# A decoder trunk on one core: early zero fills, bias ahead of the gates on VectorE, replicas in buffers of their own

## What is computed

```python
def conformer_conv(x, w1, b1, dw, dwb, g, bn, w2, b2):
    h = x @ w1 + b1
    a, gate = jnp.split(h, 2, axis=-1)
    h = a * jax.nn.sigmoid(gate)
    h = lax.conv_general_dilated(h, dw[:, None, :], window_strides=(1,),
        padding=[(CONV_WIDTH - 1, 0)], feature_group_count=D_MODEL, ...) + dwb
    h = jax.nn.silu(layer_norm(h, g, bn))
    return h @ w2 + b2

x = layer_norm(ALPHA * x + conformer_conv(x, ...), g, b)      # ALPHA = (2 * DEPTH) ** 0.25
```

## Time and profile before

| | us |
|---|---|
| median of 3 runs | 1181.94 |
| lowest and highest run | 1174.9, 1182.1 |
| span of the profiled execution, first to last instruction | 1188.2 |
| TensorE busy | 953.6 (80%) |
| VectorE busy | 454.7 (38%) |
| GpSimd busy | 221.3 (19%) |
| ScalarE busy | 169.3 (14%) |

### The profile page before, as it was taken

The page is one execution under the profiler, slowest core; times in us unless marked ns, Lnnn a source line. Parts: engine busy times, 40 slices in busy tenths (PEclk is TensorE's granted clock), DMA queues, the critical chain, the costliest instruction groups (busy, mean ns, idle before and its releaser), DMA issues.

```text
span 1188.2 us, 13863 instructions
## 1 busy us (share of the span) xinstructions
PE 953.6 (80%) x5241; PEld 495.3 (42%) x5241; DVE 454.7 (38%) x925; ACT 169.3 (14%) x376; POOL 221.3 (19%) x314
## 2 busy tenths in 40 slices
PE   5999969983999798996478999868459957899930
PEld 3444324542554454552234454534335534455510
DVE  1799913552111111110676448564511111111126
ACT  0000021301000000000123232432020000000010
POOL 1094000024211111200330002021240211020022
PEclk8999989875999899999579899877769989999975
DMA  8994349965999999999600003201859999999932
GB/s 257 388 410 142 87 157 412 408 248 200 345 388 408 385 376 391 383 420 401 249 1 0 1 1 142 71 1 50 324 200 389 378 366 384 381 389 392 395 127 106
DMA packets 82494, 313.40 MB, mean 264 GB/s; under 512 B 8798, under 2 KB 19210, under 8 KB 74089
## 3 DMA queue, kind: packets, MB, share of 16 engines
q1 hardware_dynamic: 44944, 228.83, 50.8%
q10 hardware_dynamic: 27352, 55.35, 12.4%
q0 software_dynamic: 10112, 28.06, 6.8%
HBM read 252.48 MB, written 55.31 MB: 259 GB/s over the span
## 4 chain that ended last, share of the span: by engine, by line
PE 57%; DMA 18%; DVE 14%; issue 4%; POOL 2%; ACT 2%; SPq 1%; POOLq 0%; ACTq 0%; DVEq 0%
PE ps L604 20%; PE ps L614 10%; DVE arena L858 7%; PE ps L710 6%; PE ps L729 5%; PE ps L549 5%; DMA wring<-in_moe_w_up_dram 5%; DMA wring<-in_moe_w_gate_dram 5%; DMA arena<-in_moe_w_up_dram 3%; PE ps L507 2%; DMA wring<-in_conv_w_dram 1%; DMA arena<-xs_dram,place_i 1%; DMA xs_dram<-x_sb,place_i 1%; PE ps L755 1%; PE ps L767 1%
## 5 line engine op out<-in xcount | busy, mean ns | idle before, releaser
L604 PE MATMUL ps<-wring,arena 128*64 128x256 f32 x2016 | 241.2, 396 | 54.8 <-DVE arena L1010 31.2
L604 PEld LDWEIGHTS ps<-wring,arena 128*64 128x64 f32 x2016 | 149.6, 143 | 147.0 <-issue 57.8
L1525 POOL DMA_DIRECT2D arena<-xs_dram x172 | 91.6, 538 | 358.4 <-DVE arena L1010 334.9
L614 PE MATMUL ps<-wring,arena 128*64 128x512 f32 x560 | 126.7, 594 | 6.2 <-DVE arena L1045 5.7
L507 PE MATMUL ps<-arena,wring 128*128 128x512 f32 x256 | 112.1, 600 | 5.3 <-DMA wring<-in_conv_w_dram 5.3
L1031 DVE COPY arena<-ps 128x256 f32<-128x256 f32 x32 | 13.6, 425 | 237.2 <-PE ps L647 237.2
L858 DVE SCALAR_TENSOR_TENSOR arena<-arena,dwT 128x512 f32<-128x512 f32 x116 | 96.1, 902 | 0.0
L710 PE MATMUL ps<-wring,arena 128*128 128x512 f32 x192 | 90.9, 631 | 3.5 <-ACT arena L1373 3.5
L604 PE MATMUL ps<-arena 128*64 128x256 f32 x736 | 84.7, 385 | 9.1 <-DMA arena<-in_moe_w_up_dram 7.6
L1511 POOL TENSOR_TENSOR rstd<-vareps,half 128x1 f32<-128x1 f32 x20 | 25.7, 1287 | 284.3 <-DVE vareps L874 284.3
L507 PEld LDWEIGHTS ps<-arena,wring 128*128 128x128 f32 x256 | 49.1, 193 | 66.8 <-issue 66.8
(11 more groups left out here) (189 smaller groups left out, 896.3 us busy)
## 6 DMA issues: line engine op xcount, KB each, us to landing
wring<-in_moe_w_gate_dram SPq DMA_DIRECT2D x24, 2048.0 KB, 26.4
wring<-in_moe_w_up_dram SPq DMA_DIRECT2D x24, 2048.0 KB, 19.9
wring<-in_moe_w_down_dram SPq DMA_DIRECT2D x24, 2048.0 KB, 21.3
xs_dram<-zero ACTq DMA_DIRECT2D x2, 16384.0 KB, 64.5
arena<-in_moe_w_up_dram SPq DMA_DIRECT2D x8, 2048.0 KB, 28.0
arena<-in_moe_w_down_dram SPq DMA_DIRECT2D x8, 2048.0 KB, 19.5
arena<-in_moe_w_gate_dram SPq DMA_DIRECT2D x8, 2048.0 KB, 24.7
arena<-xs_dram POOLq DMA_DIRECT2D x172, 64.0 KB, 6.4
```

The lines of the kernel that those rows point to most:

```text
L604: mm = pe.matmul(ps[h * CAP:(h + 1) * CAP, bank, 0:256], act[:, k, :], w[:, k, h * 256:(h + 1) * 256], start=(k == 0), stop=(k == KD - 1))
L614: mm = pe.matmul(ps[h * CAP:(h + 1) * CAP, bank, :], act[:, j % 2, (j // 2) * CAP:(j // 2 + 1) * CAP], w[:, j, h * 512:(h + 1) * 512], sta ...
L1525: pool.dma_start(where[q * QROWS:(q + 1) * QROWS, :, :], xs_tiles[q, :, bass.ds(n, 1), :, :]).then_inc(signal, 16)
```

## The change

- First loads: SyncE waits for the last tile of x before it issues the weights of column tile 1. ScalarE loads only the tap columns that VectorE needs, in two pieces of 16 and 15 rows; the bias row is issued right behind the tap loads.
- VectorE divides the bias row by ALPHA and adds it to the four x tiles, ahead of the parameter copies; the factor ALPHA moves into the later addition of the product, in both layers. GpSimd's scale and addition in layer 0 go; in layer 1 GpSimd divides the row once and only adds it per tile.
- Both zero fills are issued one behind the other, after the first sigmoid.
- The replicas of all four tiles have places of their own in the three slots, so they wait for their gate alone; of tile 7, ScalarE issues eight and SyncE eight.
- The gates stand at other taps, and gate 7 behind the last tile.

```diff
             conv_in(0, 1)
+            sp.wait_ge(s_x[T - 1], 16)
             conv_in(1, 1)
...
-            replicate(4)
-            replicate(5)
-            sp.wait_ge(s_g1, KD)
-            replicate(6)
-            sp.wait_ge(s_pec, 1)
-            replicate(7)
+            for c in range(DVE_TILES, KD):
+                replicate(sp, c, (0, 1) if c == KD - 1 else (0, 1, 2, 3))
...
+        FIT = KD * F // REPW
+        def shifted(c, q):
+            slot_of, at = divmod(SHIFTS * (c - DVE_TILES) + q, FIT)
+            return wring[:, 1 + slot_of, at * REPW:(at + 1) * REPW]
...
+            dve.wait_ge(s_b2, 16)
+            own(dve.tensor_scalar(resrow, resrow, 1.0 / ALPHA, None, ALU.mult))
+            for t in range(T):
+                ins = dve.tensor_tensor(x_sb[:, t, :], x_sb[:, t, :], resrow, ALU.add)
+            own(ins)
...
-            taps(1, {4: 2, 22: 3})
-            taps(2, {7: 4, 26: 5})
-            taps(3, {10: 6, 28: 7})
+            taps(1, {5: 2, 24: 3})
+            taps(2, {11: 4, 29: 5})
+            taps(3, {16: 6})
+            glu(7)
...
-                    ins = dve.tensor_tensor(x_sb[:, t, h * 512:(h + 1) * 512], x_sb[:, t, h * 512:(h + 1) * 512],
-                                            ps[:, bank + h, :], ALU.add)
+                    ins = dve.scalar_tensor_tensor(out=half_x, in0=half_x, scalar=ALPHA, in1=ps[:, bank + h, :],
+                                                   op0=ALU.mult, op1=ALU.add)
...
-            act.dma_start(dw_r[:, :], conv_dw[0]).then_inc(s_small, 16)
+            act.dma_start(dw_r[0:16, taken_cols], conv_dw[0, 0:16, taken_cols]).then_inc(s_small, 16)
+            act.dma_start(dw_r[16:CW, taken_cols], conv_dw[0, 16:CW, taken_cols]).then_inc(s_small, 16)
...
+            act.dma_start(resrow, conv_b2[0].partition_broadcast(P)).then_inc(s_b2, 16)
...
-                clear_rows(0)
+                for i in range(2):
+                    act.dma_start(xs_halves[i], zero[:, :].unsqueeze(1).to_broadcast([P, E * S // P, 512])
+                                  ).then_inc(s_xinit, 16)
...
+                if c == KD - 1:
+                    replicate(act, c, (2, 3))
...
-            clear_rows(1)
...
-            pool.wait_ge(s_x0T, T)
-            pool.wait_ge(s_rows, 16 * 8)
-            for t in range(T):
-                own(pool.tensor_scalar(x_sb[:, t, :], x_sb[:, t, :], ALPHA, None, ALU.mult))
-                pool.tensor_tensor(x_sb[:, t, :], x_sb[:, t, :], resrow, ALU.add).then_inc(s_xa, 1)
```

More of the change, by code:

```diff
@@ L239, in trunk @@
         s_pecv = sem("s_pecv")
-        s_xa = sem("s_xa")
+        s_b2 = sem("s_b2")
         s_At = sem("s_At")
@@ L358, in trunk, with replicate @@
         wdw = wring[:, 0, :].rearrange("p (r g n) -> p r g n", r=ROUNDS, g=SHIFTS * (KD - DVE_TILES))
-        def shifted(c):
-            slot_of = (1, 2, 3, 1)[c - DVE_TILES]
-            return wring[:, slot_of, 0:SHIFTS * REPW].rearrange("p (g n) -> p g n", g=SHIFTS)
+        FIT = KD * F // REPW
+        def shifted(c, q):
+            slot_of, at = divmod(SHIFTS * (c - DVE_TILES) + q, FIT)
+            return wring[:, 1 + slot_of, at * REPW:(at + 1) * REPW]
+        def replicate(eng, c, shifts):
+            eng.wait_ge(s_glu, c + 1)
+            for s in shifts:
+                for q in range(SHIFTS):
+                    eng.dma_start(shifted(c, q)[s * GRP:(s + 1) * GRP, :],
+                                  hpad[q * GRP:(q + 1) * GRP, c, s:s + REPW]).then_inc(s_rep[c - DVE_TILES], 16)
         def slot(i, *dims):
@@ L486, in parameters @@
             def parameters():
-                pe.wait_ge(s_small, 16 * 6)
+                pe.wait_ge(s_small, 16 * 7)
                 pe.transpose(ps[:, 5, 0:NPRM], prm[:, :], ident[0:NPRM, 0:NPRM])
@@ L522, in _ @@
                                          wdw[:, r, SHIFTS * (c - DVE_TILES) + q, :],
-                                         shifted(c)[:, q, SHIFTS * r:SHIFTS * r + S],
+                                         shifted(c, q)[:, SHIFTS * r:SHIFTS * r + S],
                                          start=(r == 0), stop=(r == ROUNDS - 1))
@@ L898, in add_product @@
                 for h in range(2):
[L899 to L900 removed]
+                    half_x = x_sb[:, t, h * 512:(h + 1) * 512]
+                    ins = dve.scalar_tensor_tensor(out=half_x, in0=half_x, scalar=ALPHA, in1=ps[:, bank + h, :],
+                                                   op0=ALU.mult, op1=ALU.add)
                 ins.then_inc(signal, 1)
@@ L977, in table @@
                                   ALU.mult)
-            dve.wait_ge(s_rows, 16 * 8)
+            dve.wait_ge(s_rows, 16 * 7)
             n = 0
@@ L1140, in take @@
                     half_x = x_sb[:, t, h * 512:(h + 1) * 512]
-                    dve.tensor_tensor(half_x, half_x, ps[:, bank, :], ALU.add).then_inc(bank_read[bank - 5], 1)
+                    dve.scalar_tensor_tensor(out=half_x, in0=half_x, scalar=ALPHA, in1=ps[:, bank, :],
+                                             op0=ALU.mult, op1=ALU.add).then_inc(bank_read[bank - 5], 1)
                     if h == 1 and t == T - 1:
@@ L1456, in _ @@
             pool.memset(hpad[:, :, 0:CW - 1], 0.0).then_inc(s_pool0, 1)
-            pool.wait_ge(s_small, 16 * 6)
+            pool.wait_ge(s_small, 16 * 7)
             pool.tensor_copy(pos_f[:, :], pos_i[:, :]).then_inc(s_rope, 1)
@@ L1583, in _ @@
             pool.wait_ge(s_rows1, 16 * 5)
+            own(pool.tensor_scalar(resrow, resrow, 1.0 / ALPHA, None, ALU.mult))
             def residual(t):
```

5 lines of the change are left out of this document (1 added, 4 removed).

## The result

The changed kernel is slower: 1197.92 us median (1194.29 to 1204.55, 4 runs) against 1180.01 of the kernel before on the same chip (1174.9 to 1182.1, 4 runs). The ratio is 1.014, 95% interval 1.010 to 1.019. The forecast was 1175.0, its range 1165 to 1197. What came is rival (b), whose own time, 1198, lay just outside that range.

What follows compares the result with a forecast made beforehand. It took the end of the depthwise products (166.97 us) as the bound, with TensorE and VectorE level and the fills holding tile 7; 6.3 + 0.6 = 6.9 us off the 1181.94 median gave 1175.0, range 1165 to 1197.

Steps and rivals of the forecast that it cites:

- rival (b): ScalarE stands at the second fill's issue from 44 to near 92; depthwise end 183.6, 1198 us; chance 0.15.
- Reading of the bound: Depthwise stage: the change touches nothing on the chain from 167 to 288, so the depthwise products' end, 166.97, decides.
- Part 1: First loads: first weights come with x, start 3.8 us earlier, plus 2.0 without idle time's clock cost; 5.7 in all.
- Part 2: x and bias: some 6 us on VectorE in idle time, taken 0 cost; GpSimd loses 25.4 us of work.
- Part 3: Replicas start at each gate, 0.64 us each; with ScalarE's half in time the depthwise end is 154.1, 12.9 us earlier.
- Tiles 4 to 6 are there before TensorE asks: Replicas: copies of these tiles are ready before TensorE wants them at 126.4, 133.3 and 140.3.
- Part 4: Early fills: ScalarE's queue empties between 148.4 and 155.8, taken 151; TensorE idles 3.8 us, depthwise end 160.7, gain 6.3.
- rival (a): Fills out of the way in time, TensorE runs through to 154.1: gain 12.9 + 0.6, 1168.4 us; chance 0.23.
- the forecast's own case: Both fills early without a stand: depthwise end 160.7 instead of 167.0, gain 6.3 us.
- The term that I held to decide: ScalarE's eight tile 7 replicas queue behind both fills and land near 151, so TensorE idles 3.8 us.
- Part 5: Attention: GpSimd drops four scales and gets one; gain 0 to 1.5 us, taken 0.6.
- The best corner: Whole sum at its best: no wait, start 1.3 us sooner, 0.9 more in attention; gain 16.4, 1165.5 us.

Runs made afterwards that it cites:

- experiment 1: Changed kernel with only the second fill put back behind the four depthwise bias operations: 1172.82 us against 1182.58 before, ratio 0.991.
- experiment 3: Changed kernel with the second fill issued behind the sixth sigmoid: 1194.26 us against 1182.58 before, ratio 1.013.
- experiment 5: Changed kernel with each fill cut into eight pieces of 1024 rows, all issued at the same place: 1236.78 us against 1185.23 before, ratio 1.043.
- experiment 10: Changed kernel with the second fill issued from GpSimd's queue behind the rotary steps: 1192.96 us against 1183.76 before, ratio 1.010.
- experiment 9: experiment 1 with replicas as in the kernel before (three buffers, all on SyncE, old waits): 1173.83 us against 1183.76 before, ratio 0.992.
- experiment 2: Kernel before with only the second fill moved, issued right behind the first: 1209.4 us against 1182.58, ratio 1.026.
- experiment 11: Kernel before with only the new first loads: 1176.11 us against 1183.76, ratio 0.992.
- experiment 7: experiment 1 with the first loads as in the kernel before: 1177.42 us against 1185.23 before, ratio 0.994.
- experiment 8: experiment 1 with x and bias row on GpSimd and gates' places as before: 1174.42 us against 1185.23 before (0.989); again 1169.27 against 1183.76 (0.988).
- experiment 6: Changed kernel with fill rows of 8 KB instead of 2 KB, 2048 rows a fill, same bytes: 1187.96 us against 1185.23 before, ratio 1.003.

## Why the prediction was wrong

**Reading of the bound: right.** The depthwise end carries the result nearly one for one: -10.0 there and -9.8 in time (experiment 1), +16.6 and +17.9 (the change), +10.0 and +11.7 (experiment 3), +52.1 and +51.6 (experiment 5), +9.2 and +9.2 (experiment 10). The largest differences are 5.2 (experiment 9, -4.7 and -9.9) and 3.6 (experiment 2, +23.2 and +26.8), within the 7 us by which one kernel's later stages differ from profile to profile.

**Part 1: right in kind, at most as large as taken.** Taken 5.7 us, 3.8 at the start and 2.0 of clock. In the changed kernel 2.9 at the start (19.16 to 16.23) and 1.7 in the first tile (15.70 to 14.00), 4.6; alone (experiment 11) 5.5 at the depthwise end; taken out again (experiment 7) 2.9. The first products now wait for VectorE's copy of the transposed x and no longer for weights. The second term is not sure to come: with the new first loads and an idle time of 1.4 to 1.5 us ahead of it, the first tile took 14.00 in the changed kernel and in most experiments, but 15.6 to 15.7 in experiments 1, 5 and 9. In 1 and 9 the granted clock was 1.00 all through that tile, so the clock does not explain it all, and the rest is open.

**Part 2: right as a cost, and worth nothing.** The additions lie in VectorE's idle time (16.8 to 23.1 us in the changed kernel, ahead of its parameter copies near 31) and the undisturbed gates came within 0.2 us of the forecast's in experiment 10. But with x on GpSimd and the replicas in their own buffers TensorE does not wait either (experiment 8).

**Part 3: right where no fill runs.** At the depthwise end 4.8 us with x on VectorE (experiment 9 against 1) and 6.8 with x on GpSimd: 145.7 us from TensorE's start to that end in experiment 11, 138.9 in experiment 8, and the medians, on one chip, differ by 6.8 too. "Tiles 4 to 6 are there before TensorE asks" failed beside the fills.

**Part 4: wrong in two steps.** The first is the argument against (b): "SyncE passed its second load behind a first one in 0.7 us and stood from the third on, and ACT has one fill ahead of the second". It counted transfers. Experiment 6 shows that rows count: with a quarter of the rows and all the bytes the stand falls from 45.0 to 27.5 us, and experiment 5 that even 1024 rows ahead, behind the small row loads, are enough. A fill has 8192; the first load that SyncE's second one passed was 512 KB in rows of 512 bytes, 1024 of them, an eighth of that. I had the price of this rival to the microsecond (depthwise end 183.6, 1198), and gave it 0.15 on that row.

The match at 183.6 is in part luck. ScalarE came free at 88.1 and not at 92, so the gates were about 4 us sooner than (b) had them; the replicas beside the rest of fill 2 took part of that back: tile 4's products began 18.3 us after its gate at 127.89, where sixteen undisturbed copies need 12.2. From there SyncE issued its 56 copies without a break, so the delay reached tile 6, whose products began at 167.97 where (b) had 169.8:

```profile
128.66 42.82 SPq L372 DMA_DIRECT2D wring<-arena  x56
```

The last 128 products then took 15.64 us and not 13.9, at a granted clock of 0.66 on the mean of 167 to 172 us, and that is the other part.

The second step would have failed without a stand as well. I priced the replicas by bytes, as what they take from the fill (10.8 to 18.2 us), and let each still be issued in 0.64 us. Beside a fill one takes 1.64 to 1.75 us to issue and 7.5 to 8 to land (experiments 3 and 10), 26 us and more for a tile's sixteen. With the gates on time the end is then 177.0 (experiment 3, one fill at a time) or 176.2 (experiment 10, two side by side) and not 160.7: the forecast's own case comes out 9 to 10 us slower at that end, not 6.3 faster. So rival (a) failed by the same step, and either of the two settles the sign. Experiment 6 shows them together: its stand of 27.5 us is shorter than the 30 from which the forecast let the gain turn, and the end is still 5.9 us late.

The term that I held to decide, ScalarE's eight replicas behind both fills, never came up in the changed kernel: by its last gate at 165 the fills had been done for 25 us. Where it did (experiment 3), the copies did not lie quietly in the queue but held ScalarE 26 us at their issue.

**Part 5: taken 0.6, open.** The later stages differ by up to 7 us from one profile of the same kernel to the next (582.9 and 575.7, experiment 8's kernel), so neither 0 nor 4 us is excluded. The best corner of the sum is added up wrongly: 12.9 + 1.3 + 0.6 + 0.9 is 15.7 and not 16.4, so it stands at 1166.2; nothing hangs on it.

**What early fills could have won** was nothing to begin with: the forecast itself priced GpSimd's wait for the second fill at 0, and experiment 1 keeps that wait (24.8 us) and is 2.3% of the time of before faster than the changed kernel (0.991 against 1.014).

What stays open: why small copies on another queue go so slowly beside a fill (by packet, by queue or in some other way) was not tried apart; a fill with 8 KB rows slows a replica as much (1.60 us, 15 issues in 111 to 135 of experiment 6), so the rows' length is not it. Whether experiment 8's version really beats experiment 1's is not settled.

## What to carry to other kernels

Issuing a transfer was cheap here only when little was left in its queue: ask of every DMA what is ahead of it in the same queue, in rows, and whose next compute instruction stands behind the issue. A background transfer is not free for small latency-bound copies beside it, even where the bandwidth is there; price those by their issue and landing time under load. And if the early end of a transfer is worth nothing, leave it where nothing waits.

## What the runs showed of the hardware beyond that

- The engine that issues a second transfer stood until some 900 to 1500 rows ahead of it were left: 1160 (changed kernel, rows of 2 KB), 920 (experiment 6, rows of 8 KB), 1500 (experiment 5, pieces of 1024 rows), estimates from landing times. The first fill, with only small loads ahead, took 0.66 us to issue at 8192 rows and at 2048.
- The rows' length did not change the speed of a fill: 8192 rows of 2 KB landed in 53.2 us, 2048 of 8 KB in 51.4.
- Two fills at once from two queues (ScalarE's at 42.0, GpSimd's at 64.9) shared the engines and landed at 150.1 and 148.5, some 8 to 10 us later than behind each other (140.6), perhaps in part for the copies beside them, which was not tried apart. GpSimd paid 2.99 us for the issue of 8192 rows.
- A replica of 67.5 KB beside a fill: 1.64 us to issue and 7.5 to land against 0.59 and 2.0.
